# Strassen's scheme for twelve channel tiles of the down-projections, with GpSimd making low parts of token blocks

## The reference

```python
def conv_ffn(h, w_up, conv_w, conv_b, w_down):
    gate, val = jnp.split(h @ w_up, 2, axis=-1)
    gate = lax.conv_general_dilated(...) + conv_b      # causal, depthwise, width 3
    return (jax.nn.silu(gate) * val) @ w_down          # (512, 2816) @ (2816, 1024)
```

## Time and profile before

| | us |
|---|---|
| Median of 3 runs (1188.20 to 1188.35) | 1188.32 |
| The profiled execution, its own time | 1188.03 |
| Its span on the core | 1186.2 |
| PE busy in the span | 1174.4 (99%) |
| Nine units of the down-projection, layer 0 (432 matmuls) | 98.18 |
| The same, layer 1 | 98.16 |

### The profile page before, as it was taken

The page is one execution under the profiler, slowest core; times in us unless marked ns, Lnnn a source line. Parts: engine busy times, 40 slices in busy tenths (PEclk is TensorE's granted clock), DMA queues, the critical chain, the costliest instruction groups (busy, mean ns, idle before and its releaser), DMA issues.

```text
span 1186.2 us, 21327 instructions
## 1 busy us (share of the span) xinstructions
PE 1174.4 (99%) x7666; PEld 1076.9 (91%) x7670; DVE 746.1 (63%) x1318; ACT 637.3 (54%) x1003; POOL 681.3 (57%) x593
## 2 busy tenths in 40 slices
PE   8999999999999999999999999999999999999997
PEld 7999999889999999988888889978999999998886
DVE  7888777658787777723241375644877787762325
ACT  6665555537665656532343365444766565653334
POOL 2434445326877777666645331611787777766672
PEclk9999999999999999999999999999999999999999
DMA  7232222122332322332223211411233232323221
GB/s 267 100 107 71 90 89 72 36 71 72 115 112 94 110 101 106 125 107 73 104 77 120 106 72 37 142 37 36 75 139 106 98 113 88 113 102 107 92 85 71
DMA packets 17334, 113.83 MB, mean 96 GB/s; under 512 B 1920, under 2 KB 2304, under 8 KB 4608
## 3 DMA queue, kind: packets, MB, share of 16 engines
q1 hardware_dynamic: 16416, 110.20, 26.1%
q10 hardware_dynamic: 864, 2.88, 0.7%
HBM read 110.98 MB, written 2.10 MB: 95 GB/s over the span
## 4 chain that ended last, share of the span: by engine, by line
PE 95%; DVE 2%; ACT 1%; issue 1%; DMA 0%; DVEq 0%; ACTq 0%
PE ps L2118 34%; PE ps L2166 17%; PE ps L1911 9%; PE ps L1768 7%; PE ps L1802 3%; PE ps L1830 3%; PE ps L2299 2%; PE ps L1952 2%; PE ps L1875 2%; PE ps L2279 2%; PE ps L1819 2%; PE ps L1880 1%; PE ps L2203 1%; PE ps L1938 1%; PE ps L1710 1%
## 5 line engine op out<-in xcount | busy, mean ns | idle before, releaser
L350 POOL TENSOR_TENSOR w_lo<-w_raw,w_hi 128x512 fp32r<-128x512 f32 (+2 forms) x169 | 256.9, 1551 | 277.5 <-ACT w_hi L474 221.6
L408 POOL TENSOR_TENSOR w_lo<-w_raw,w_hi 128x512 fp32r<-128x512 f32 x120 | 152.9, 1297 | 85.1 <-ACT w_hi L745 66.6
L474 ACT ACTIVATE w_hi<-w_raw 128x2048 fp32r<-128x2048 f32 (+1 forms) x53 | 95.5, 1801 | 166.4 <-PE ps L2166 129.4
L408 POOL TENSOR_TENSOR s_lo<-s_raw,s_hi 128x512 fp32r<-128x512 f32 x120 | 154.9, 1322 | 0.0
L1454 DVE TENSOR_TENSOR hT_lo<-region,hT_hi 128x2048 fp32r<-128x2048 f32 (+1 forms) x22 | 58.9, 2685 | 138.6 <-ACT hT_hi L821 138.6
L2166 PE MATMUL ps<-w_hi,hT_hi 128*128 128x512 f32 x288 | 112.2, 390 | 0.3
L2166 PE MATMUL ps<-w_hi,hT_lo 128*128 128x512 f32 x288 | 112.0, 389 | 0.0
L2166 PE MATMUL ps<-w_lo,hT_hi 128*128 128x512 f32 x288 | 112.0, 389 | 0.0
L745 ACT ACTIVATE w_hi<-w_raw 128x1536 fp32r<-128x1536 f32 x40 | 59.5, 1488 | 71.8 <-PE ps L2118 71.8
L2118 PE MATMUL ps<-hT_hi,w_hi 128*128 128x256 f32 x320 | 90.8, 284 | 0.0
L2118 PE MATMUL ps<-hT_hi,w_lo 128*128 128x256 f32 x320 | 90.6, 283 | 0.0
(11 more groups left out here) (329 smaller groups left out, 3603.0 us busy)
## 6 DMA issues: line engine op xcount, KB each, us to landing
w_raw<-weights SPq DMA_DIRECT2D x99, 1024.0 KB, 4.8
gain<-gains ACTq DMA_DIRECT2D x4, 512.0 KB, 4.2
x<-x_in SPq DMA_DIRECT2D x3, 512.0 KB, 7.3
out<-region SPq DMA_DIRECT2D x3, 512.0 KB, 2.6
w_raw<-weights SPq DMA_DIRECT2D x2, 384.0 KB, 5.5
w_raw<-weights SPq DMA_DIRECT2D x1, 768.0 KB, 8.5
cst<-consts SPq DMA_DIRECT2D x1, 640.0 KB, 10.3
x<-x_in ACTq DMA_DIRECT2D x1, 512.0 KB, 4.3
```

What stands on the lines that cost most here:

```text
L350: ins = pool.tensor_tensor(w_lo[:, slot, cols], w_raw[:, slot, cols], w_hi[:, slot, cols].bitcast(f32), ALU.subtract)
L408: return pool.tensor_tensor(dst, raw, high.bitcast(f32), ALU.subtract)
L474: sc.activation(w_hi[:, slot, 0:used], w_raw[:, slot, 0:used], ACT.Copy).then_inc(w_hi_ready, 1)
```

## The change

For channel tiles 0 to 11 the down-projection is done in six steps. A step takes two channel tiles (r = 0, 1), both halves of the columns (c = 0, 1) and the tokens in two halves of 256, that is a product of 2x2 by 2x2 blocks. Before, it was eight block products of 2 token tiles x 3 passes = 6 matmuls each; now it is seven, by Winograd's form of Strassen's scheme, with S1 to S4 as sums of activation blocks and T1 to T4 as sums of weight blocks. The channel tiles 12 to 21 stay as they were. In units of `w_raw`:

- X units (0 to 5), one step each, 1536 columns (B11, B12, B22; 768 KB): three products, A11 by B11 to banks 0 and 1, S1 by T1 to banks 2 and 3, S3 by T3 to banks 4 and 5.
- Z units (6 to 8), two steps each, 2048 columns: two products per step, A12 by B21 and S4 by B22, to banks 6, 7, 2 and 3.
- Y units (9 to 11), two steps each, 2048 columns: two products per step, S2 by T2 and A22 by T4, to banks 0, 1, 6 and 7. T3 of each step was kept in SBUF during the X units.
- Plain units (12 to 16), as before; `last_two` runs on 15 and 16.

So a layer has 17 units and 17 transfers instead of 11, and 492 matmuls instead of 528. The banks are emptied into `x` by DVE after unit 5 (four additions of 512 columns, six of 1024), after unit 8 and after unit 11. POOL makes S1 and S2 in the loop over pairs (`act_sums`), and in the down-projection (`down_lows`) the low parts of A11|S1 in each X unit (the first phase's token blocks), those of S2 and A22 in the Y units, and of nearly all weights; DVE makes S3, S4, T1 to T4, and the low parts of S3, A12, S4, T1 and T2. ACT copies B12 and T3 to PSUM (`stage_b12`, `stage_t3`) and makes all high parts. SP asks for a unit, as before, once `w_lo_ready` has counted the unit two before it.

```diff
+            load_range(2, W_DN0)
+            for n1, after in ((W_DN0, W_DN1), (W_DN1, W_ALL)):
+                for m in range(n1, n1 + 6):
+                    sp.wait_ge(w_lo_ready, m - 1)
+                    load(m, m % 2, 1536)
+                load_range(n1 + 6, after)
...
+                def act_sums(i):
+                    a11, s1, a22 = act[:, ds(2 * i - 2, 1), 0:256], act[:, ds(2 * i - 2, 1), 256:512], act[:, ds(2 * i - 1, 1), 256:512]
+                    pool.wait_ge(act_done[l], 2 * i)
+                    pool.tensor_tensor(s1, s1, a22, ALU.add).then_inc(act_summed[l], 1)
+                    pool.wait_ge(act_summed[l], 2 * i - 1)
+                    pool.tensor_tensor(s2_raw[:, ds(i - 1, 1), :], s1, a11, ALU.subtract).then_inc(act_summed[l], 1)
...
+            def down_lows(l, n1):
+                for u in X_UNITS:
+                    slot, row = u % 2, 2 * (u % 4)
+                    pool.wait_ge(a_highs[l], 2 * u + 1)
+                    low(hT_lo[:, row, :], act[:, 2 * u, :], hT_hi[:, row, :]).then_inc(first_rows_low[l], 1)
+                    pool.wait_ge(b11_high[l], u + 1)
+                    low(w_lo[:, slot, 0:512], w_raw[:, slot, 0:512], w_hi[:, slot, 0:512]).then_inc(b11_low[l], 1)
+                    pool.wait_ge(w_hi_ready, n1 + u + 1)
+                    low(w_lo[:, slot, 1024:1536], t3_of(u), w_hi[:, slot, 1024:1536]).then_inc(w_lo_ready, 1)
+                for u in Z_UNITS:
+                    slot = u % 2
+                    pool.wait_ge(w_hi_ready, n1 + u + 1)
+                    for n in range(len(STEPS[u])):
+                        for c in (1024 * n, 1024 * n + 512):
+                            ins = low(w_lo[:, slot, c:c + 512], w_raw[:, slot, c:c + 512], w_hi[:, slot, c:c + 512])
+                        if n == 0:
+                            ins.then_inc(step_low[l], 1)
+                    ins.then_inc(w_lo_ready, 1)
...
             # ACT, after the last pair
+                for u in range(1, 6):
+                    x_unit_highs(u)          # b11_hi(u), t1_t3_hi(u), sum_hi_of(u)
+                    if u == 2:
+                        load_gain()
+                    if u < 5:
+                        stage_b12(u + 1)
+                        a11_s1_hi(u + 1)
+                z_tokens_hi(6)
+                for u in Z_UNITS:
+                    z_weights_hi(u)
+                    if u < 8:
+                        z_tokens_hi(u + 1)   # the second of its two waits for s4(u + 1)
...
             # DVE, after the last pair
+                for u in range(1, 6):
+                    t1_t3(u)
+                    s3(u)
+                    t1_low(u)
+                    s3_low(u)
+                for u in (6, 7):
+                    s4(u)
+                    z_lows(u)
+                after_unit(5, 0)
+                for t in range(2):
+                    add(t, 1, 2 + t)
+                    ins = add(2 + t, 1, 2 + t)
+                ins.then_inc(x_added[l], 1)
+                ve.wait_ge(x_added[l], 1)
+                for t in range(2):
+                    add_both(t, t)
+                    ins = add_both(2 + t, t)
+                ins.then_inc(x_added[l], 1)
+                ve.wait_ge(x_added[l], 2)
+                for t in range(2):
+                    ins = add_both(2 + t, 4 + t)
+                ins.then_inc(x_added[l], 1)
+                s4(8)
+                z_lows(8)
...
             # PE
+                for u in X_UNITS:
+                    row, slot = 2 * (u % 4), u % 2
+                    pe.wait_ge(b11_low[l], u + 1)
+                    pe.wait_ge(first_rows_low[l], u + 1)
+                    down_product(row, 0, slot, 0, 0, u == 0, u == 5)
+                    pe.wait_ge(t_lows[l], u + 1)
+                    down_product(row, 256, slot, 512, 2, u == 0, u == 5)
+                    if u == 0:
+                        pe.wait_ge(act_done[l], 2 * PAIRS)
+                    pe.wait_ge(w_lo_ready, n1 + u + 1)
+                    pe.wait_ge(a_lows[l], u + 1)
+                    down_product(row + 1, 0, slot, 1024, 4, u == 0, u == 5).then_inc(mm_done, 4)
+                for u in Z_UNITS:
+                    row, slot = 2 * (u % 4), u % 2
+                    pe.wait_ge(a_lows[l], 6 + 2 * (u - 6) + 2)
+                    pe.wait_ge(step_low[l], u - 6 + 1)
+                    for p, n in ((2, 0), (2, 1), (3, 0), (3, 1)) if u == 6 else ((2, 0), (3, 0), (2, 1), (3, 1)):
+                        if n and p == 2:
+                            pe.wait_ge(w_lo_ready, n1 + u + 1)
...
+                for u in Y_UNITS:
+                    for n, j in enumerate(STEPS[u]):
+                        pe.wait_ge(t_lows[l], 6 + j + 1)
+                        down_product(row, 256 * n, slot, 1024 * n, 0, j == 0, j == 5)
...
+                pe.wait_ge(w_lo_ready, n1 + 13)
+                pe.wait_ge(act_lo[l], 4)
+                plain_part(12, 0, (0, 1, 2, 3), 0, first=True)
```

More of the change, by code:

```diff
@@ L38 @@
 W_DN0 = W_UP0 + FT
-W_DQK = W_DN0 + FT // 2
+DOWN = 17
+W_DQK = W_DN0 + DOWN
 W_DV = W_DQK + 2
@@ L2156, in mlp @@
                 block_tile(LAST, 1, last=True)
-                def down_tile(slot, parts, last, wait_w, wait_lo):
-                    pe.wait_ge(w_lo_ready, wait_w)
-                    pe.wait_ge(act_lo[l], wait_lo)
-                    for c, units, first, stop, incs in parts:
-                        for t in range(NT):
-                            for u in units:
-                                for n, (h, w) in enumerate(PASSES):
-                                    ins = pe.matmul(ps[:, 4 * c + t, :], h[:, 4 * slot + u, t * 128:(t + 1) * 128],
-                                                    w[:, slot, u * 512:(u + 1) * 512],
-                                                    start=first and u == units[0] and n == 0,
-                                                    stop=stop and u == units[-1] and n == 2)
-                            if incs[t]:
-                                ins.then_inc(mm_done, incs[t])
@@ L2183, in mlp, with down_product @@
-                for j in (6, 7, 8):
-                    down_tile(j % 2, [(1, four, False, False, every)], False, n1 + j + 1, 4 * (j + 1))
-                pe.wait_ge(act_lo[l], 40)
-                last_two(n1 + 9, (4, False), (0, False), lambda: pe.wait_ge(act_lo[l], 44))
+                def down_product(row, a0, slot, c, bank, first=False, last=False):
+                    for t in range(2):
+                        for n, (h, w) in enumerate(PASSES):
+                            ins = pe.matmul(ps[:, bank + t, :], h[:, row, a0 + 128 * t:a0 + 128 * t + 128], w[:, slot, c:c + 512],
+                                            start=first and n == 0, stop=last and n == 2)
+                    return ins
@@ new lines, in plain_part @@
+                def plain_part(u, c, rows, k0, first=False, last=False, incs=1):
+                    for t in (2, 3, 0, 1):
+                        if first and c == 0 and t < 2:
+                            pe.wait_ge(x_added[l], 6 + t)
+                        for k, row in enumerate(rows, k0):
+                            for n, (h, w) in enumerate(PASSES):
+                                ins = pe.matmul(ps[:, 4 * c + t, :], h[:, row, t * 128:(t + 1) * 128],
+                                                w[:, u % 2, k * 512:(k + 1) * 512], start=first and k == k0 and n == 0,
+                                                stop=last and k == k0 + len(rows) - 1 and n == 2)
+                        if incs == 1:
+                            ins.then_inc(mm_done, 1)
+                    if incs == 2:
+                        ins.then_inc(mm_done, 2)
```

408 lines of the change are left out of this document (328 added, 80 removed).

## The result

The changed kernel takes **1213.63 us**, median of 4 runs (1213.38 to 1215.89), against 1188.26 of the kernel before in the same session: 25.4 us slower, ratio 1.0218, 95% interval 1.0200 to 1.0236. The forecast was 1207, range 1191 to 1216.

The account below looks back on a forecast made before the run. PE bounded the kernel, busy 99% of the span. Per layer 17.4 us of waits on the weights' feed against 8.16 saved gave 9.3 more, so 1188.03 + 18.6 = 1206.6, said as 1207; range 1191 to 1216.

Parts of the forecast that it names:

- The saving: Down-projection: 36 of 528 matmuls fewer per layer at 0.2267 us each, 8.16 us, 16.3 us for both layers.
- The waits: PE waits per layer in X, Z and Y units and ahead of unit 12: 17.4 us against 8.16 saved.
- end of X: PE ends unit 5 at 529.1 in layer 0, 6.4 us later than the 522.7 without waits.
- unit 8 starts: Unit 8 starts at 545.5 after a PE wait of 2.4 us, S4 standing behind ten additions on DVE.
- the round trip: X units, one slot: handover 0.17, load 4.5, ACT 1.2, POOL 4.3; 10.2 us per two units, against PE's 4.08 per unit.
- the sign "under 4 us": Sign that the forecast is wrong: X units' loads of 768 KB landing in under 4 us; 4.5 was assumed.
- The wait of 1.1 for the last activations: Unit 0 of X: PE's third product waits 1.1 us for DVE's last activations, ready at 502.0.
- The price of the port: POOL loses 2.04 us beside DVE's 2048 columns; forecast took 0.5 per X unit, 1.0 for 1024 columns.
- Rival 3: Granted clock falls in PE's waits: 2 us per fall, two falls per layer, 8 more, 1215; chance 0.13.
- Rival 1: Feed of weights keeps up, only the wait for the last activations stays: faster, 1174; chance 0.10.
- Rival 2: Half of the waits, X at POOL's pace of 4.3: 2.6 more per layer, 1193; chance 0.17.
- Costed at nothing: Terms priced at zero, among them POOL's S1 and S2 in the up-projection's six pairs, at most 0.74 us each.

Follow-up runs that it names:

- filled wait: Changed kernel plus 34 small matmuls of a mask, result unused, on PE in the wait ahead of unit 12: 1210.69 us, ratio 1.0185.
- the last two experiments: Changed kernel with POOL making 64 of each 512 columns of X, Z and unit 12 low parts: 1187.23 us; plus early loads and S4 ahead of additions: 1185.05 us.
- early loads and halves together: Changed kernel with early loads, unit 12's split before rows, unit 8's S4 and lows earlier, weights handed on in halves, DVE making X rows' low parts: 1205.26 us.
- S4 first: Changed kernel, but DVE makes S4 of unit 8 before the ten additions to x: 1212.71 us, ratio 1.0199.
- small low parts: Changed kernel, but POOL makes only 64 of each 512 columns of weights' low parts in X, Z and unit 12: 1187.23 us, ratio 0.9989.
- DVE's rows: Changed kernel, but DVE instead of POOL makes the low parts of A11|S1 in the X units: 1214.75 us, ratio 1.0217.
- links in halves: Changed kernel with early loads, unit 12's split before rows, unit 8's S4 and lows earlier, weights of units 6, 7, 8, 12 handed on in halves: 1206.69 us.

## Why the prediction was right, and where it was off

**The saving** of 72 matmuls at 0.2267 us each: the count holds. With POOL's pieces made small and the time lost in the stage counted, the sum with it meets the measured time (1186.1 and 1186.0).

**The waits**, layer 0, in us of the profile (in layer 1 unit 12 starts 75.5 us after X, here 75.3):

| step | forecast | measured |
|---|---|---|
| end of X | 529.1 | 526.6 |
| Z6 starts | 530.5 | 530.12 |
| unit 8 starts | 545.5 | 545.78 |
| unit 10 starts | 557.8 | 558.37 |
| unit 12 starts | 572.7 | 573.46 |
| units 12 to 14 | 32.6 | 35.51 |

**X** was paced by the round trip, and PE was released by POOL's B11 piece, as said. POOL's last pieces of units 1 to 5 end at 504.6, 508.8, 514.0, 519.8 and 523.9 (forecast 505.9, 510.3, 516.1, 520.5, 526.3). Three round trips took 9.4, 11.0 and 9.9 us, a mean of 10.1 against 10.2. That the mean meets the forecast is in part luck: the loads of units 3 and 5 landed in 4.01 and 3.96 us, not 4.5 (in layer 1 two in 3.91 and 3.98, so the sign "under 4 us" was just touched), but unit 4's took 5.62, beside ACT's load of a gain, and so the three come to 4.5 in the mean. PE's starts of the X units are 4.1, 5.0, 5.3, 5.8 and 4.1 us apart, 4.9 in the mean, not evenly 4.7 to 5.3. The wait of 1.1 for the last activations did not come, since DVE had written them at 500.6 and not at 502.0, just before PE's third product. The chain through X is also not POOL's alone, as my sum had it: POOL's last piece of unit 2 and the load are in it, but then ACT's staging, DVE's T3 and T1, ACT's highs and DVE's sums up to S4 of unit 6.

```profile
507.47 1.30 POOL w_lo L435
508.79 5.62 DMA w_raw<-weights
514.43 0.61 ACT ps L873
515.06 0.70 DVE region L1606
```

X ended 2.5 us before its forecast, but that did not help: Z6's weights have their own chain (asked for at 519.97, landed 4.7 us later), and the wait ahead of it was 3.4 instead of 1.4. ACT's and POOL's timelines of the changed kernel:

```profile
524.52 0.64 ACT L897 ACTIVATE hT_hi<-hT_raw 128x512 fp32r<-128x512 f32 x1 [2.21 <-DVE hT_raw L1636]
525.05 1.90 ACT L920 ACTIVATE w_hi<-w_raw 128x2048 fp32r<-128x2048 f32 x1
...
540.59 0.64 ACT L897 ACTIVATE hT_hi<-hT_raw 128x512 fp32r<-128x512 f32 x1 [9.20 <-DVE hT_raw L1636]
541.12 1.90 ACT L920 ACTIVATE w_hi<-w_raw 128x2048 fp32r<-128x2048 f32 x1
...
565.33 1.92 ACT L554 ACTIVATE w_hi<-w_raw 128x2048 fp32r<-128x2048 f32 x1 [0.25 <-DMA w_raw<-weights]
```
```profile
522.46 1.47 POOL L435 TENSOR_TENSOR w_lo<-region,w_hi 128x512 fp32r<-128x512 f32 x1
...
567.33 12.06 POOL L377 TENSOR_TENSOR w_lo<-w_raw,w_hi 128x512 fp32r<-128x512 f32 x8 [1.97 <-ACT w_hi L554]
```

Unit 6's weights are split until 526.95 (forecast 527.5), POOL's two pieces follow. ACT's row at 540.59 is unit 8: idle 9.20 us for DVE's S4, as forecast. At 565.33 ACT had waited for the load, and POOL's first four of eight pieces in a row, 1.5 us each, set the start of unit 12. The price of the port (2.04 us per 2048 columns in the earlier trace rows, a quarter of it per X unit) held: POOL's X pieces took 1.45 to 1.50 us beside DVE and 1.29 alone, two per unit, so 0.4 us; ahead of unit 12 one piece of four took 2.25, the 1.0 us of the forecast. The DVE side I had left out:

```profile
501.95 0.42 DVE L1619 TENSOR_TENSOR hT_raw<-region 128x256 f32<-128x256 f32 x1
...
506.15 1.36 DVE L1619 TENSOR_TENSOR hT_raw<-region 128x256 f32<-128x256 f32 x1
...
522.70 1.78 DVE L1636 TENSOR_TENSOR hT_raw<-region 128x512 f32<-128x512 f32 x1
...
530.45 2.47 DVE L1684 TENSOR_TENSOR x<-x,ps 128x512 f32<-128x512 f32 x4
532.95 7.00 DVE L1688 TENSOR_TENSOR x<-x,ps 128x1024 f32<-128x1024 f32 x6
539.87 0.68 DVE L1636 TENSOR_TENSOR hT_raw<-region 128x512 f32<-128x512 f32 x1
```

An operation of 256 columns with both inputs in SBUF takes 0.42 us alone and up to 1.36 beside POOL. The last three rows are the ten additions, 9.5 us (forecast 9.8), and S4 behind them.

**The term that was mis-sized is the clock, costed at nothing in the sum.** Rival 3 named it at 2 us per fall, two per layer; no row stood behind that price then. The sum gave 9.3 us per layer up to unit 12; measured are 573.46 - 498.2 - 57.1 = 18.2 of delay less 8.16, so 10.0. The fall after the wait ahead of unit 12 costs 35.51 - 32.6 = 2.9 more. Twice 12.9 on 1188.03 is 1213.8; the profiled execution took 1213.4. So my mechanism with rival 3's addition in one of its two places: the fall after the wait ahead of Z6 cost PE about 2 us too (ten matmuls 0.43 apart), but unit 8 would have waited for POOL anyway. So PE waited only 0.8 us ahead of unit 8, not 2.4, and yet unit 8 started where the forecast had it. The filled wait shows the size of the other fall alone, 2.6 us per layer.

**Rival 1**, the feed that keeps up, is excluded, and the last two experiments show its price of 1174 to be out of reach for this order of work even without most of POOL's load: DVE and ACT then hold PE. **Rival 2**, half of the waits at 1193, is excluded too; early loads and halves together still leave 1205. **Costed at nothing** and found so: POOL's sums in the up-projection; the chain up to 498 has no new piece of POOL's.

## What to carry to other kernels

Before a scheme that saves matmuls is built on a kernel that PE fills, divide: each unit of weights brings nearly the same load, split and low parts as before (in X three quarters of them, and token blocks besides), and PE now eats an X unit in 4.1 us and a Z or Y unit in 5.4, where a unit took 10.9. With two slots, PE's time for two units has to cover the round trip of one slot; in X it was 8.2 us against 10.1. Where it doesn't, waits eat the saving, and taking one link out of the trip brings the next (load, ACT's order, DVE's additions) rather than the gain. A wait of PE of a few us also has a price in the slower matmuls behind it, 2.6 to 2.9 us per layer ahead of unit 12 here, and belongs in the sum.

## What the runs showed of the hardware

- **Whether the clock falls does not hang on the length of one wait alone.** All twelve waits of 4.1 to 4.8 us ahead of unit 12, in six kernels, were followed by 7 to 13 matmuls 0.43 us apart, a fall to 1.2 GHz. Between 1.9 and 3.5 us it went both ways: a fall behind a wait of 2.0 at unit 8 (S4 first) and of 2.2 in X (filled wait), none behind 2.6 at unit 8 (small low parts, both layers) nor behind 3.34, 3.36 and 3.44 ahead of Z6 (S4 first, filled wait, DVE's rows; layer 0), where the changed kernel fell after 3.36. No single wait of 1.8 us or less had slow matmuls behind it unless a longer one had just gone before. The Trainium skill, "TensorE: Matmul & The Clock Gate", section on the HAM oscillation, says that idle gaps between groups of matmuls take the clock down; the trace now agrees, with this spread. The place of the falls differs from profile to profile, which fits the scatter of these kernels' times by 1.4 to 5.7 us where the kernel before stays within 1.4. With the links in halves the execution of 1203.6 us has a mean granted clock of 0.995 and that of 1209.3 one of 0.988, with the small low parts 1185.2 has 0.999 and 1188.6 has 0.995; in other kernels the order is less clear, and that the falls make all of the scatter is not shown.
- **Beside each other POOL and DVE slow both.** With both inputs of each in SBUF, POOL's piece of 512 columns went from 1.29 to 1.50 us beside DVE's short operations and to 2.25 beside its 1024 columns, DVE's 256 columns from 0.42 to 1.36, and its 1024 columns took 2.06 on the average in place of about 1.2. The short operation of DVE loses most in proportion. The one of 1.36 us started inside a piece of POOL's and ended 0.28 us after it (507.52 and 507.24).
- **Small matmuls that keep the clock are worth more than they cost here**: 34 of them in a wait of 4 us bought 2.6 us of the matmuls behind it, 2.9 us of the whole time for the two layers.
